# Two-layer trunk on one core: the order of the wide and narrow products inside a k-tile of the feed-forward layers

## The chip, the core and the metric

The kernel runs on one core of a Trainium2 chip. The metric is the device time of one execution in microseconds (us), and of several executions the median is taken. TensorE (PE in the profile) multiplies, and its weight loads are shown apart as PEld; VectorE (DVE), ScalarE (ACT) and GpSimd (POOL) do the element-wise work; SyncE (SP) issues the weight transfers.

## What is computed

The input x is 256 tokens of width 2048 in float32. Two residual layers follow each other, each with a mixer and a feed-forward part, and a final norm ends it. The feed-forward part is where the change lies:

```python
def conv_ffn(h, w_up, conv_w, conv_b, w_down):
    u = jnp.einsum('bsd,df->bsf', h, w_up)          # 2048 -> 11264
    S = u.shape[1]
    y = conv_b
    for tap in range(CONV_WIDTH):
        shifted = jnp.pad(u, ((0, 0), (tap, 0), (0, 0)))[:, :S]
        y = y + shifted * conv_w[CONV_WIDTH - 1 - tap]
    val, gate = jnp.split(y, 2, axis=-1)
    return jnp.einsum('bsf,fd->bsd', jax.nn.silu(gate) * val, w_down)   # 5632 -> 2048

    for l in range(DEPTH):                          # DEPTH = 2
        h = rms_norm(x, mix_norm[l])
        x = x + (parallel_mixer(h, ...) if l % 2 == 0 else pool_mixer(h, ...))
        h = rms_norm(x, ffn_norm[l])
        x = x + conv_ffn(h, w_up[l], conv_w[l], conv_b[l], w_down[l])
    return rms_norm(x, final_norm)
```

## The kernel before

Activations lie feature-major, 128 features on the partitions and 256 tokens (S) along the free axis. Every float32 operand is split in two parts of the type fp32r: a rounded part and the rest. For the weights these are the tiles `hi` (ScalarE, line 727) and `lo` = raw - hi (VectorE, line 1082). For the activations both parts stand side by side in one row of 512 columns, in `h` for the up-projection and in `act` for the down-projection.

A product of a 128x128 block of weights with the activations therefore takes two matmuls. The **wide** one (line 386) multiplies the `hi` block with all 512 columns and writes a whole PSUM bank. The **narrow** one (line 388) multiplies the `lo` block with the first 256 columns and adds to the second half of the same bank. Lo times lo is left out.

A **k-tile** is 128 rows of a weight matrix by 512 columns, so it has four blocks m = 0..3, four banks and eight matmuls. A unit is four k-tiles (KT = 4), which one transfer of 1 MB brings into one of four slots of `raw`. `hi` and `lo` hold one unit each. ScalarE rounds k-tile kt of the next unit when the semaphore `w_used` says that TensorE has done k-tile kt of this one, VectorE then subtracts, and TensorE waits on `lo_done` before each k-tile. `w_used` rises with the last matmul of a k-tile.

In the function `wide_unit` TensorE sends the eight matmuls of a k-tile in alternation: wide 0, narrow 0, wide 1, narrow 1, and so on. It serves the output projection of the first mixer (64 k-tiles), both up-projections (11 pairs of column groups, each 2 x 4 units of 4 k-tiles, so 352 k-tiles for a layer) and both down-projections (4 column groups of 11 units, so 176 k-tiles for a layer). The very last unit is sent by `last_unit` in an order of its own. That makes 352 + 176 k-tiles in the feed-forward part of layer 0 and 352 + 172 in that of layer 1 through `wide_unit`, 1052 together. Two accumulators of four banks alternate from one column group to the next.

Three other orders occur in the kernel. The input projection's queries and keys use `half_unit` (lines 436 and 438), which also alternates wide and narrow. Its value groups and the pool mixer use `token_unit` (lines 468, 470, 471): only matmuls with 512 moving columns, each with another block of weights than the one before. The first group uses `narrow_unit` (lines 452, 454, 455): only matmuls with 256 moving columns. A weight load precedes every matmul.

The up-projections run in a hardware loop over pairs, the down-projection of layer 0 in a loop over two halves; that of layer 1 is written out.

Of the kernel before, what the change touches and what calls it, by code (L numbers as in the profile page):

```python
# [29 lines left out]
P = 128  # L30
# [4 lines left out]
KT = 4  # L35


def trunk_kernel(nc, xT, rel_bias, norm_g, w_in, w_out, lam, subln, pool_w, pool_scale,
                 w_up, conv, w_down, bucket_onehot, rot_cos, rot_sin, decay, pool_matrix, ident_in, flip_in, outT):
    D, S = xT.shape  # L40
# [6 lines left out]
    DN_UNITS = FF // COLS  # L47
    DN_GROUPS = D // COLS
# [65 lines left out]
    with ctx:  # L114
# [174 lines left out]
        def wide_bank(G):  # L289

            return 4 - 4 * (G % 2)
# [83 lines left out]
        def _(pe):  # L375
            def wide_unit(n, base, bank, first, last, moving, ready=None):

                for kt in range(KT):

                    pe.wait_ge(lo_done, base + KT * n + kt + 1)  # L380
                    if ready is not None:
                        ready(kt)
                    mv = moving(kt)
                    for m in range(4):
                        c = slice(m * P, (m + 1) * P)
                        pe.matmul(ps[:, bank + m, :], hi[:, kt, c], mv, start=first and kt == 0, stop=False,  # L386
                                  skip_group_check=True)
                        mm = pe.matmul(ps[:, bank + m, S:2 * S], lo[:, kt, c], mv[:, 0:S], start=False,  # L388
                                       stop=last and kt == KT - 1, skip_group_check=True)
                    mm.then_inc(w_used, 1)  # L390

            def last_unit(n, bank):
# [244 lines left out]
            for l in range(DEPTH):  # L637
                if l == 1:
                    def pool_tokens(g):

                        pe.wait_ge(z_ready, 2 * (g + 1))
                        if g == 0:
                            pe.wait_ge(table_in, 16 * N_TABLE)
                        if g == 1:
                            pe.wait_ge(rms_done, 3)
                        if g >= 2:
                            pe.wait_ge(evacuated, G_POOL + g - 1)
                        z, b = (yv, yg)[g % 2], wide_bank(G_POOL + g) + 2
                        z = z.rearrange("p (t k) s -> p t (k s)", t=2)
                        for m in range(4):  # L650
                            c = slice(m * P, (m + 1) * P)
                            out = ps[:, b + m // 2, (m % 2) * S:(m % 2 + 1) * S]
                            pe.matmul(out[:, 0:NEAR], z[:, 0, c], pool_m[:, g, 0:NEAR], start=m % 2 == 0, stop=False,
                                      skip_group_check=True)
                            mm = pe.matmul(out[:, P:2 * P], z[:, 1, c], pool_m[:, g, S:S + P], start=False, stop=True,
                                           skip_group_check=True)
                        mm.then_inc(pooled_mm, 1)

                    for g in range(4):
                        G = G_POOL + g
# [12 lines left out]
                    pool_tokens(3)  # L675

                def up(i, first):
                    for gt in range(2):
                        G = G_UP[l] + gt
                        pe.wait_ge(evacuated, i * 2 + G - 1)  # L680
                        for j in range(UP_UNITS):
                            def split(kt):
                                pe.wait_ge(h_lo, H_BASE[2 * l + 1] + KT * j + kt + 1)
                            wide_unit(U_UP[l] + 4 * gt + j, i * (8 * KT), wide_bank(G), j == 0, j == UP_UNITS - 1,
                                      lambda kt: h[:, KT * j + kt, :], split if first and gt == 0 else None)
                            if first and gt == 1 and j == 0:
# [8 lines left out]
                def down(i, half, units):  # L695
                    G = G_DN[l] + half
                    pe.wait_ge(evacuated, i * 2 + G - 1)
                    for j in range(units):
                        pe.wait_ge(act_lo, l * PAIRS + j + 1)
                        wide_unit(U_DN[l] + DN_UNITS * half + j, i * (2 * DN_UNITS * KT), wide_bank(G), j == 0,  # L700
                                  j == DN_UNITS - 1, lambda kt: act[:, KT * j + kt, :])

                if l == 0:
                    with pe.Fori(0, DN_GROUPS // 2) as i:
                        down(i, 0, DN_UNITS)
                        down(i, 1, DN_UNITS)
                else:
                    down(0, 0, DN_UNITS)
                    down(0, 1, DN_UNITS)
                    down(1, 0, DN_UNITS)  # L710
                    down(1, 1, DN_UNITS - 1)
# [915 lines left out]
```

## Time and profile before

| | us |
|---|---|
| median of 3 runs | 1962.93 |
| lowest and highest of them | 1962.78, 1976.23 |
| the profiled execution | 1979.08 |
| its span, first to last instruction | 1976.9 |
| busy: PE, DVE, ACT | 1955.4, 1391.7, 1112.8 |

The profile is of one execution, and its own time is 2.2 us longer than its span. A row of the page groups instructions by line, engine and operation: the mean duration of one, the idle time of the engine ahead of them, and what ended it. Matmuls are pipelined, so one that lasts 395 ns in the records can be followed by the next after 233 ns. What a matmul costs is the distance from its start to the next start, called its slot here. The timeline gives starts to 0.01 us, and a slot is best read over several matmuls, or from how many of a kind fall into a stretch.

### The profile page before, as it was taken

The page shows a single profiled execution, that of the slowest core. Times are in us where ns is not written, and L with a number is a line of the kernel's source. Part 1 is how long each engine was busy: PE and PEld are TensorE (multiplying, and loading weights), DVE is VectorE, ACT ScalarE, POOL GpSimd, SP SyncE. Part 2 cuts the span into 40 slices and gives each one's busy share as a digit, 9 for nine tenths or more (in the row PEclk, how much of TensorE's full clock was granted, in tenths as well). Part 3 has the DMA queues.
Part 4 walks back from the last instruction along what each step waited for, and adds up shares of the span by engine and source line. Part 5 has one row for each costly group of instructions (what it writes and reads, how often), then busy time and mean ns, then how long its engine had stood idle before and what let it go on. Part 6 is the DMA issues. An engine that isn't in the chain of part 4 may idle for free.

```text
span 1976.9 us, 31335 instructions
## 1 busy us (share of the span) xinstructions
PE 1955.4 (99%) x11094; PEld 1699.6 (86%) x11094; DVE 1391.7 (70%) x2149; ACT 1112.8 (56%) x1844; POOL 48.2 (2%) x53
## 2 busy tenths in 40 slices
PE   8999999999999999999999999999999999999998
PEld 8888888888888888888888888888888888888887
DVE  6667776767777777777655555877777777755555
ACT  6555545556655666665544445666666656645554
POOL 0002240000000000000000000000000000000000
PEclk9999999999999999999999999999999999999999
DMA  9655555555555555554565554555555555555653
GB/s 321 192 170 164 177 168 164 180 191 186 181 187 191 184 180 188 191 182 159 191 213 181 181 169 150 171 191 191 191 191 191 188 186 187 187 167 191 212 192 107
DMA packets 205203, 364.91 MB, mean 185 GB/s; under 512 B 6564, under 2 KB 49101, under 8 KB 205133
## 3 DMA queue, kind: packets, MB, share of 16 engines
q1 hardware_dynamic: 203388, 362.34, 55.6%
q10 hardware_dynamic: 1744, 1.63, 0.3%
q8 instruction: 46, 0.75, 0.2%
q14 instruction: 25, 0.20, 0.0%
HBM read 361.83 MB, written 2.11 MB: 184 GB/s over the span
## 4 chain that ended last, share of the span: by engine, by line
PE 97%; DVE 2%; ACT 1%; issue 0%; DMA 0%; DVEq 0%; SPq 0%
PE ps L386 53%; PE ps L388 26%; PE ps L436 6%; PE ps L438 3%; PE ps L468 2%; PE ps L471 2%; PE ps L470 2%; DVE lo L1082 1%; PE ps L452 0%; PE ps L454 0%; PE ps L455 0%; ACT hi L727 0%; PE ps L561 0%; PE ps L575 0%; DVE ssq L1200 0%
## 5 line engine op out<-in xcount | busy, mean ns | idle before, releaser
L1082 DVE TENSOR_TENSOR lo<-raw,hi 128x512 fp32r<-128x512 f32 x1360 | 927.8, 698 | 528.7 <-ACT hi L727 524.1
L727 ACT ACTIVATE hi<-raw 128x512 fp32r<-128x512 f32 x1352 | 844.9, 631 | 807.3 <-PE ps L388 672.1
L386 PE MATMUL ps<-h,hi 128*128 128x512 f32 x2816 | 988.5, 397 | 4.8 <-DVE x L1389 3.3
L388 PE MATMUL ps<-h,lo 128*128 128x256 f32 x2816 | 786.5, 279 | 0.0
L386 PEld LDWEIGHTS ps<-h,hi 128*128 128x128 f32 x2816 | 529.4, 188 | 133.6 <-DVE x L1389 3.5
L388 PEld LDWEIGHTS ps<-h,lo 128*128 128x128 f32 x2816 | 531.1, 189 | 0.0
L386 PE MATMUL ps<-act,hi 128*128 128x512 f32 x1392 | 487.3, 396 | 0.0
L388 PE MATMUL ps<-act,lo 128*128 128x256 f32 x1392 | 388.3, 279 | 0.0
L386 PEld LDWEIGHTS ps<-act,hi 128*128 128x128 f32 x1392 | 261.3, 188 | 63.1
L388 PEld LDWEIGHTS ps<-act,lo 128*128 128x128 f32 x1392 | 262.2, 188 | 0.0
L436 PE MATMUL ps<-h,hi 128*128 128x512 f32 x576 | 205.4, 400 | 1.0 <-DVE lo L1082 1.0
L438 PE MATMUL ps<-h,lo 128*128 128x256 f32 x576 | 160.9, 279 | 0.0
L436 PEld LDWEIGHTS ps<-h,hi 128*128 128x128 f32 x576 | 108.1, 188 | 27.2 <-DVE lo L1082 2.1
L438 PEld LDWEIGHTS ps<-h,lo 128*128 128x128 f32 x576 | 108.6, 189 | 0.2
L386 PE MATMUL ps<-mixed,hi 128*128 128x512 f32 x256 | 90.5, 399 | 0.0
L388 PE MATMUL ps<-mixed,lo 128*128 128x256 f32 x256 | 71.9, 281 | 0.0
L468 PE MATMUL ps<-hi,h 128*128 128x512 f32 x160 | 64.4, 403 | 1.2 <-DVE lo L1082 1.0
L470 PE MATMUL ps<-lo,h 128*128 128x512 f32 x160 | 62.9, 393 | 0.0
L471 PE MATMUL ps<-hi,h 128*128 128x512 f32 x160 | 62.9, 393 | 0.0
L1335 DVE TENSOR_TENSOR u<-u,ps 128x1024 f32<-128x1024 f32 x44 | 53.8, 1222 | 9.7 <-ACT u L913 9.7
L386 PEld LDWEIGHTS ps<-mixed,hi 128*128 128x128 f32 x256 | 48.1, 188 | 12.1
L1340 DVE TENSOR_TENSOR u<-u,rstd 128x1024 f32<-128x1024 f32 x44 | 53.9, 1226 | 1.5
(175 smaller groups left out, 1122.4 us busy)
## 6 DMA issues: line engine op xcount, KB each, us to landing
raw<-in_w_up SPq DMA_DIRECT2D x176, 1024.0 KB, 5.0
raw<-in_w_down SPq DMA_DIRECT2D x88, 1024.0 KB, 5.1
raw<-in_w_in SPq DMA_DIRECT2D x54, 1024.0 KB, 5.2
raw<-in_w_out SPq DMA_DIRECT2D x16, 1024.0 KB, 5.0
raw<-in_pool_w SPq DMA_DIRECT2D x4, 1024.0 KB, 5.2
raw<-in_w_in SPq DMA_DIRECT2D x8, 256.0 KB, 4.8
x<-in_xT SPq DMA_DIRECT2D x8, 128.0 KB, 4.6
x<-in_xT SPq DMA_DIRECT2D x2, 512.0 KB, 7.7
```

What stands on the lines that cost most here:

```text
L386: pe.matmul(ps[:, bank + m, :], hi[:, kt, c], mv, start=first and kt == 0, stop=False, skip_group_check=True)
L388: mm = pe.matmul(ps[:, bank + m, S:2 * S], lo[:, kt, c], mv[:, 0:S], start=False, stop=last and kt == KT - 1, skip_group_check=True)
L436: pe.matmul(acc[:, m, :], hi[:, kt, c], mv, start=first and kt == 0 and a == 0, stop=False, skip_group_check=True)
L438: mm = pe.matmul(acc[:, m, S:2 * S], lo[:, kt, c], mv[:, 0:S], start=False, stop=last and kt == KT - 1 and a == 1, skip_group_check=True)
L468: pe.matmul(acc[:, t, :], xh, hi[:, kt, :], start=first and kt == 0, stop=False, skip_group_check=True)
L470: pe.matmul(acc[:, t, :], xh, lo[:, kt, :], start=False, stop=False, skip_group_check=True)
L471: mm = pe.matmul(acc[:, t, :], xl, hi[:, kt, :], start=False, stop=last and kt == KT - 1, skip_group_check=True)
L727: a_.activation(hi[:, kt, :], raw[:, slot, kt, :], ACT.Copy).then_inc(hi_done, 1)
L1082: ve.tensor_tensor(lo[:, kt, :], raw[:, slot, kt, :], hi[:, kt, :].bitcast(F32), ALU.subtract).then_inc(lo_done, 1)
L1335: ve.tensor_tensor(u[:, :, :], u[:, :, :], ps[:, b:b + 4, S:2 * S], ALU.add).then_inc(evacuated, 1)
L1340: ve.tensor_tensor(u[:, :, :], u[:, :, :], rstd_4, ALU.mult).then_inc(u_ready, 1)
```

## The change

The change keeps all matmuls, their operands and their banks. It sets for each stage of the feed-forward layers in which order the eight matmuls of a k-tile are sent. Seven small functions write such orders, and `ordered_unit` takes one of them as an argument. With W for wide and N for narrow, they are:

| order | the eight matmuls | where | k-tiles |
|---|---|---|---|
| rows_then_singles | W0 W1 N0 N1 W2 N2 W3 N3 | up, layer 0 | 352 |
| rows_of_two | W0 W1 N0 N1 W2 W3 N2 N3 | up, layer 1; down, layer 1, groups 1 and 3 | 352 + 44 + 40 |
| folded_end | W0 N0 W1 N1 W2 N2 N3 W3 | down, layer 0 group 0, layer 1 group 2 | 88 |
| row_of_three | W0 W1 W2 N0 N1 N2 W3 N3 | down, layer 0 group 1 | 44 |
| one_ahead | W0 W1 N0 W2 N1 N2 W3 N3 | down, layer 0 group 2 | 44 |
| narrow_first | N0 W0 N1 W1 N2 W2 N3 W3 | down, layer 0 group 3 | 44 |
| one_and_three | W0 N0 W1 W2 W3 N1 N2 N3 | down, layer 1 group 0 | 44 |

In the first k-tile of a group, folded_end and narrow_first keep the old order, since there the wide matmul has to start the bank.

```diff
+            def rows_then_singles(bank, kt, mv, start):
+                wide(bank, kt, 0, mv, start)
+                wide(bank, kt, 1, mv, start)
+                narrow(bank, kt, 0, mv)
+                narrow(bank, kt, 1, mv)
+                wide(bank, kt, 2, mv, start)
+                narrow(bank, kt, 2, mv)
+                wide(bank, kt, 3, mv, start)
+                narrow(bank, kt, 3, mv).then_inc(w_used, 1)
...
+            def rows_of_two(bank, kt, mv, start):
+                for row in (0, 2):
+                    wide(bank, kt, row, mv, start)
+                    wide(bank, kt, row + 1, mv, start)
+                    narrow(bank, kt, row, mv)
+                    mm = narrow(bank, kt, row + 1, mv)
+                mm.then_inc(w_used, 1)
+
+            def ordered_unit(n, base, bank, first, moving, tile, ready=None):
+
+                for kt in range(KT):
+                    pe.wait_ge(lo_done, base + KT * n + kt + 1)
+                    if ready is not None:
+                        ready(kt)
+                    tile(bank, kt, moving(kt), first and kt == 0)
...
-                            wide_unit(U_UP[l] + 4 * gt + j, i * (8 * KT), wide_bank(G), j == 0, j == UP_UNITS - 1,
-                                      lambda kt: h[:, KT * j + kt, :], split if first and gt == 0 else None)
+                            ordered_unit(U_UP[l] + 4 * gt + j, i * (8 * KT), wide_bank(G), j == 0,
+                                         lambda kt: h[:, KT * j + kt, :], (rows_then_singles, rows_of_two)[l],
+                                         split if first and gt == 0 else None)
...
+                down_tiles = ((folded_end, row_of_three, one_ahead, narrow_first),
+                              (one_and_three, rows_of_two, folded_end, rows_of_two))[l]
+                for g in range(DN_GROUPS):
+                    G = G_DN[l] + g
+                    pe.wait_ge(evacuated, G - 1)
+                    for j in range(DN_UNITS - (l == 1 and g == 3)):
                         pe.wait_ge(act_lo, l * PAIRS + j + 1)
-                        wide_unit(U_DN[l] + DN_UNITS * half + j, i * (2 * DN_UNITS * KT), wide_bank(G), j == 0,
-                                  j == DN_UNITS - 1, lambda kt: act[:, KT * j + kt, :])
...
+                        ordered_unit(U_DN[l] + DN_UNITS * g + j, 0, wide_bank(G), j == 0,
+                                     lambda kt: act[:, KT * j + kt, :], down_tiles[g])
```

The down-projection of layer 0 is also written out now, as that of layer 1 was. What the other engines do and their order stay as they were. On TensorE, one k-tile of an up-projection stood like this before (`lo_done` is the semaphore of the tile's `lo` part; REGISTER_ALU works out the value to wait for in the loop):

```order
L380 REGISTER_ALU
L386 MATMUL ps<-h,hi 128x512 [waits lo_done]
L388 MATMUL ps<-h,lo 128x256
L386 MATMUL ps<-h,hi 128x512
L388 MATMUL ps<-h,lo 128x256
L386 MATMUL ps<-h,hi 128x512
L388 MATMUL ps<-h,lo 128x256
L386 MATMUL ps<-h,hi 128x512
L388 MATMUL ps<-h,lo 128x256
```

Wide and narrow alternate through the k-tile and across its border. In the up-projection of layer 0 one k-tile and the start of the next now read (L394 wide, L399 narrow):

```order
L394 MATMUL ps<-h,hi 128x512 [waits lo_done]
L394 MATMUL ps<-h,hi 128x512
L399 MATMUL ps<-h,lo 128x256 x2
L394 MATMUL ps<-h,hi 128x512
L399 MATMUL ps<-h,lo 128x256
L394 MATMUL ps<-h,hi 128x512
L399 MATMUL ps<-h,lo 128x256
L394 MATMUL ps<-h,hi 128x512 [waits lo_done]
L394 MATMUL ps<-h,hi 128x512
```

One narrow has moved behind the next wide, so a wide now follows a wide once and a narrow a narrow once; the other six places are as before. In the up-projection of layer 1 the same piece of TensorE's program reads:

```order
L473 REGISTER_ALU
L394 MATMUL ps<-h,hi 128x512 [waits lo_done]
L394 MATMUL ps<-h,hi 128x512
L399 MATMUL ps<-h,lo 128x256 x2
L394 MATMUL ps<-h,hi 128x512 x2
L399 MATMUL ps<-h,lo 128x256 x2
L473 REGISTER_ALU
L394 MATMUL ps<-h,hi 128x512 [waits lo_done]
```

Here both happen twice. In the down-projection of layer 0, group 0 (folded_end; L421 is the last wide), two k-tiles meet like this:

```order
L394 MATMUL ps<-act,hi 128x512
L399 MATMUL ps<-act,lo 128x256 x2
L421 MATMUL ps<-act,hi 128x512
L394 MATMUL ps<-act,hi 128x512 [waits lo_done,act_lo]
L399 MATMUL ps<-act,lo 128x256
```

The wide that ends one k-tile is followed by the wide that begins the next, and `w_used` now rises with a wide.

## Rows read from the trace of the kernel before

**Rows 1.** The page: busy us (share) xinstructions; PE's granted clock in 40 slices, tenths

```profile
PE 1955.4 (99%) x11094; PEld 1699.6 (86%) x11094; DVE 1391.7 (70%) x2149; ACT 1112.8 (56%) x1844; POOL 48.2 (2%) x53
PEclk9999999999999999999999999999999999999999
PE 97%; DVE 2%; ACT 1%; issue 0%; DMA 0%; DVEq 0%; SPq 0%
```

**Rows 2.** The page's costliest groups: busy us, mean ns | idle before, releaser

```profile
L386 PE MATMUL ps<-h,hi 128*128 128x512 f32 x2816 | 988.5, 397 | 4.8 <-DVE x L1389 3.3
L388 PE MATMUL ps<-h,lo 128*128 128x256 f32 x2816 | 786.5, 279 | 0.0
L386 PE MATMUL ps<-act,hi 128*128 128x512 f32 x1392 | 487.3, 396 | 0.0
```

**Rows 3.** Busy time of line 386 in the four feed-forward stages: us, busy (xinstructions), clock

```profile
353.00:941.00 588.00, 587.80 (x1664) 312.49 (x1663) 1.00 0.56 184
941.00:1189.00 248.00, 248.00 (x703) 131.91 (x702) 1.00 0.56 185
1262.00:1719.00 457.00, 457.00 (x1320) 247.22 (x1319) 1.00 0.57 187
1720.00:1957.00 237.00, 237.00 (x685) 128.17 (x684) 1.00 0.54 183
```

**Rows 4.** The same view of two stretches of 200 us, in layer 0 and layer 1

```profile
700.00:900.00 200.00, 200.00 (x567) 106.35 (x566) 1.00 0.57 185
1500.00:1700.00 200.00, 200.00 (x578) 108.19 (x577) 1.00 0.58 189
```

**Rows 5.** Groups by line from 1500 to 1700 us: the two engines that prepare weights

```profile
L1082 DVE TENSOR_TENSOR lo<-raw,hi 128x512 fp32r<-128x512 f32 x144 | 96.2, 689 | 38.9 <-ACT hi L727 38.9
L727 ACT ACTIVATE hi<-raw 128x512 fp32r<-128x512 f32 x145 | 90.5, 630 | 77.9 <-PE ps L388 77.9
```

**Rows 6.** Timeline of PE, layer 1's first up-projection: start us, us, line, operation

```profile
1258.16 0.40 PE L386 MATMUL ps<-h,hi 128*128 128x512 f32 x1
...
1259.22 0.60 PE L486 MATMUL ps<-sqacc,ones 128*128 128x256 f32 x2
1259.55 0.50 PE L386 MATMUL ps<-h,hi 128*128 128x512 f32 x1
...
1261.05 0.39 PE L386 MATMUL ps<-h,hi 128*128 128x512 f32 x1
...
1263.13 0.39 PE L386 MATMUL ps<-h,hi 128*128 128x512 f32 x1
```

**Rows 7.** Timeline of PE in a token_unit, matmuls of 512 columns alone

```profile
66.75 0.39 PE L468 MATMUL ps<-hi,h 128*128 128x512 f32 x1
...
69.47 0.39 PE L468 MATMUL ps<-hi,h 128*128 128x512 f32 x1
```

**Rows 8.** Timeline of PE in a narrow_unit, matmuls of 256 columns alone

```profile
19.50 0.28 PE L452 MATMUL ps<-h,hi 128*128 128x256 f32 x1
...
21.66 0.28 PE L452 MATMUL ps<-h,hi 128*128 128x256 f32 x1
```

**Rows 9.** Timeline of PE where a token_unit is followed by a half_unit

```profile
228.40 0.39 PE L471 MATMUL ps<-hi,h 128*128 128x512 f32 x1
228.63 0.39 PE L436 MATMUL ps<-h,hi 128*128 128x512 f32 x1
228.85 0.28 PE L438 MATMUL ps<-h,lo 128*128 128x256 f32 x1
228.97 0.40 PE L436 MATMUL ps<-h,hi 128*128 128x512 f32 x1
...
229.32 0.40 PE L436 MATMUL ps<-h,hi 128*128 128x512 f32 x1
...
229.68 0.40 PE L436 MATMUL ps<-h,hi 128*128 128x512 f32 x1
```

**Rows 10.** Timeline of PE where alternation is followed by a token_unit

```profile
1189.88 0.40 PE L468 MATMUL ps<-hi,h 128*128 128x512 f32 x1
1190.12 0.40 PE L470 MATMUL ps<-lo,h 128*128 128x512 f32 x1
...
1191.98 0.39 PE L468 MATMUL ps<-hi,h 128*128 128x512 f32 x1
```

More of the change, by code:

```diff
@@ L390, in wide_unit, with wide, narrow @@
                     mm.then_inc(w_used, 1)
+            def wide(bank, kt, m, mv, start=False):
+                pe.matmul(ps[:, bank + m, :], hi[:, kt, m * P:(m + 1) * P], mv, start=start, stop=False,
+                          skip_group_check=True)
+            def narrow(bank, kt, m, mv):
+                return pe.matmul(ps[:, bank + m, S:2 * S], lo[:, kt, m * P:(m + 1) * P], mv[:, 0:S], start=False,
+                                 stop=False, skip_group_check=True)
+            def rows_then_singles(bank, kt, mv, start):
[7 more added lines that the diff above has]
+                narrow(bank, kt, 3, mv).then_inc(w_used, 1)
@@ new lines, in folded_end @@
+            def folded_end(bank, kt, mv, start):
+                for m in range(3):
+                    wide(bank, kt, m, mv, start)
+                    narrow(bank, kt, m, mv)
+                if start:
+                    wide(bank, kt, 3, mv, start)
+                    narrow(bank, kt, 3, mv).then_inc(w_used, 1)
+                else:
+                    narrow(bank, kt, 3, mv)
+                    pe.matmul(ps[:, bank + 3, :], hi[:, kt, 3 * P:4 * P], mv, start=False, stop=False,
+                              skip_group_check=True).then_inc(w_used, 1)
@@ new lines, in row_of_three, with one_ahead @@
+            def row_of_three(bank, kt, mv, start):
+                for m in range(3):
+                    wide(bank, kt, m, mv, start)
+                for m in range(3):
+                    narrow(bank, kt, m, mv)
+                wide(bank, kt, 3, mv, start)
+                narrow(bank, kt, 3, mv).then_inc(w_used, 1)
+            def one_ahead(bank, kt, mv, start):
+                wide(bank, kt, 0, mv, start)
+                wide(bank, kt, 1, mv, start)
+                narrow(bank, kt, 0, mv)
+                wide(bank, kt, 2, mv, start)
+                narrow(bank, kt, 1, mv)
+                narrow(bank, kt, 2, mv)
+                wide(bank, kt, 3, mv, start)
+                narrow(bank, kt, 3, mv).then_inc(w_used, 1)
@@ new lines, in one_and_three, with narrow_first @@
+            def one_and_three(bank, kt, mv, start):
+                wide(bank, kt, 0, mv, start)
+                narrow(bank, kt, 0, mv)
+                for m in range(1, 4):
+                    wide(bank, kt, m, mv, start)
+                for m in range(1, 4):
+                    mm = narrow(bank, kt, m, mv)
+                mm.then_inc(w_used, 1)
+            def narrow_first(bank, kt, mv, start):
+                for m in range(4):
+                    if start:
+                        wide(bank, kt, m, mv, start)
+                        mm = narrow(bank, kt, m, mv)
+                    else:
+                        narrow(bank, kt, m, mv)
+                        mm = pe.matmul(ps[:, bank + m, :], hi[:, kt, m * P:(m + 1) * P], mv, start=False, stop=False,
+                                       skip_group_check=True)
+                mm.then_inc(w_used, 1)
@@ new lines, in rows_of_two @@
+            def rows_of_two(bank, kt, mv, start):
[4 more added lines that the diff above has]
+                    mm = narrow(bank, kt, row + 1, mv)
+                mm.then_inc(w_used, 1)
+            def ordered_unit(n, base, bank, first, moving, tile, ready=None):
[4 more added lines that the diff above has]
+                    tile(bank, kt, moving(kt), first and kt == 0)
@@ L694, in _ @@
                     up(i, False)
[L695 to L698, printed above, removed]
-                        pe.wait_ge(act_lo, l * PAIRS + j + 1)
-                        wide_unit(U_DN[l] + DN_UNITS * half + j, i * (2 * DN_UNITS * KT), wide_bank(G), j == 0,
-                                  j == DN_UNITS - 1, lambda kt: act[:, KT * j + kt, :])
[L703 to L711, printed above, removed]
+                down_tiles = ((folded_end, row_of_three, one_ahead, narrow_first),
[4 more added lines that the diff above has]
+                    for j in range(DN_UNITS - (l == 1 and g == 3)):
+                        pe.wait_ge(act_lo, l * PAIRS + j + 1)
+                        ordered_unit(U_DN[l] + DN_UNITS * g + j, 0, wide_bank(G), j == 0,
+                                     lambda kt: act[:, KT * j + kt, :], down_tiles[g])
+                if l == 1:
                     last_unit(U_DN[1] + DN_UNITS * DN_GROUPS - 1, wide_bank(G_DN[1] + 3))
```

## The prediction

> **What bounds the kernel now.** I read the page's engine shares first. TensorE is busy for 99% of the span, the chain that ended last lies on it for 97%, and its clock is at the full level in every slice [rows 1]. In the page's costliest groups the wide matmuls of lines 386 and 388 had 4.8 us of idle time ahead of them in all, most of it in front of one layer's start, and the narrow ones none [rows 2]. So neither a transfer nor a preparing engine sets the pace of the feed-forward parts; TensorE's own rate does. From 1500 to 1700 us, 144 or 145 k-tiles pass. VectorE idles 38.9 us for ScalarE in them, and ScalarE 77.9 us for TensorE's release of a k-tile [rows 5]. ScalarE thus waits about 0.5 us per k-tile for TensorE, never the other way round.
>
> A busy share says nothing about the rate, so I counted matmuls per stretch. A wide and a narrow make a pair, and there are four in a k-tile. From 700 to 900 us 567 wides start, 352.7 ns for a pair. From 1500 to 1700 us there are 578, 346.0 ns for a pair [rows 4]. It is the same code with the same shapes, no waits and the full clock. The four stages show that the rate goes by layer: 588.0 us / 1664 = 353.4 ns and 248.0 / 703 = 352.8 ns in layer 0, 457.0 / 1320 = 346.2 ns and 237.0 / 685 = 346.0 ns in layer 1 [rows 3]. The loop or the written-out form makes no difference: the last stage is written out, the one before it is a loop, and both run at 346.
>
> So **alternation has two steady rates**, 353 and 346 ns a pair, and keeps the one it falls into. The timeline shows it change. From 1258.16 to 1259.22 us three pairs took 1.06 us, 353 each. Then two small matmuls of line 486 interrupt the stream, and from 1261.05 to 1263.13 six pairs took 2.08 us, 346.7 each [rows 6]. What an interruption changes must be how the starts fall against something inside the engine; the trace doesn't show what.
>
> **What equal neighbours cost.** The change puts a wide behind a wide and a narrow behind a narrow, which alternation never does. The trace has both in other stages. Twelve 512-column matmuls in a row, each with another weight block, took 69.47 - 66.75 = 2.72 us, 226.7 ns each [rows 7]. Eighteen 256-column ones took 21.66 - 19.50 = 2.16 us, 120.0 ns each [rows 8]. Together that is 346.7 ns for one wide and one narrow, the faster rate of alternation. The 256 columns between the two shapes take 106.7 ns, 2.4 a nanosecond, which leaves 13.3 ns on top for each matmul of either shape. The pure streams and the good alternation pay the same.
>
> The Trainium skill, page "TensorE: Matmul & The Clock Gate", section "Back-to-back issue gap", gives N / 2.4 + 2.5 ns from start to start at the full clock, so 215.8 and 109.2 ns. The rows above, at 226.7 and 120.0, differ from it by 11 ns each. By the page's figures an equal neighbour would be cheaper than any slot this kernel shows. I go by the rows.
>
> **The change part by part.** Counting wide-to-wide places with the next k-tile's first matmul included, rows_of_two, row_of_three and one_and_three have 2 in a k-tile, rows_then_singles, one_ahead and folded_end 1, narrow_first 0. Layer 0 has 352 x 1 + 44 x (1 + 2 + 1 + 0) = 528 of them. Layer 1 has 352 x 2 + 44 x (2 + 2 + 1) + 40 x 2 = 1004. Together 1532, and as many narrow-to-narrow. Each such couple replaces a wide-to-narrow and a narrow-to-wide.
>
> *Slots.* In layer 1, which is at the faster rate, one couple costs 226.7 + 120.0 in place of 346.0, so +0.7 ns, and over all 1532 of them +1.1 us. In layer 0 I take it that the new orders do not hold the slower rate: each k-tile there breaks the alternation at least once (narrow_first apart), and the slower rate is seen only in unbroken alternation. Then 528 k-tiles x 4 pairs x (352.7 - 346.0 = 6.7 ns) = -14.2 us.
>
> *Bounds of a slot.* The nearest rows to a change of neighbours are the places where stages meet. Behind a stream of wides, the first two alternating pairs took 229.32 - 228.63 = 0.69 us, 345 each, and the third 0.36 us [rows 9]. That is the cheap end, 1.7 ns a pair under the fast rate. Behind slow alternation, a stream of wides needs ten matmuls to settle: 1191.98 - 1189.88 = 2.10 us for nine, 233.3 ns each, 6.6 over the settled 226.7 [rows 10]. That is the dear end. I take the settled price, because it agrees from three sides, and keep both ends.
>
> *k-tile's end.* narrow_first and folded_end let `w_used` rise with a wide in place of a narrow. It still is the last of the same eight, so it comes when the k-tile is through. ScalarE's half microsecond of waiting per k-tile [rows 5] covers any shift of one slot. Without that cover, a shift of 0.1 us would reach TensorE by way of `lo_done`. Cost nothing.
>
> *Written-out loop, register work.* Two groups more of TensorE's code are written out in layer 0, at nothing, as rows 3 show for layer 1.
>
> **The sum.** The profiled execution took 1979.1 us. 1979.1 - 14.2 + 1.1 = **1966.0 us**. Two of the three runs of before are at 1962.8 and one at 1976.2; the 13.4 us between them are what one layer at the slower rate costs. So the median 1962.9 is probably already a run with both layers at the faster rate, and against it the change brings +3, 0.2%. About 1% is what a measurement of this kernel can tell from no change, so this is no change.
>
> **The rivals.**
>
> *A: the mixtures fall into a slow rate of their own.* Breaking a steady alternation may as well land in the dear rate as in the cheap one: rows 6 show that an interruption decides, not which way. With 352.7 ns a pair everywhere the time is 1966.0 + 1052 x 4 x 6.7 ns = 1966 + 28 = 1994, 1.6% slower. Half of the k-tiles there, or each k-tile half way, gives 1980. For it speaks that the pairs behind a stream of wides did not stay cheap: the third took 360 ns [rows 9]. Against it speaks that two of the new orders' pieces, the pure rows, have one rate only.
>
> *B, the other side by more: the stream never settles.* In rows 10 the starts need ten matmuls to settle after a change of neighbours, and the new orders have a change of neighbours within every eight. If each slot stays 6.6 ns dear, a k-tile costs 53 ns more and the time is 1966 + 1052 x 53 ns = 2022. It turns from no change to slower where a k-tile costs more than 16 ns over 1387, since 1982.6 - 1966 = 16.6 us over 1052 k-tiles. Against it: the ladder in rows 10 starts from the slow rate, and its excess shrinks.
>
> *C: equal neighbours are cheap inside a k-tile.* Here a wide following a wide goes to another bank and keeps its moving columns, which no stage of before does; in rows 7 the bank stays. If both slots lost 10.9 ns, 1532 couples would give 1532 x 21.9 = 33 us, so 1933, and with the wides alone 1949. Those are the gaps that the Trainium skill's section "Back-to-back issue gap" gives. By rows, only the 1.7 ns a pair of rows 9 can be won: 1052 x 4 x 1.7 = 7 us, so 1959. In rows 8 three narrows share bank and weight block and still take 120, which speaks against a saving.
>
> *D: nothing changes, layer by layer.* The rate of each layer is again drawn at its start, the orders do nothing: 1963 to 1979, as before. It differs from my forecast in the trace, not in the verdict.
>
> **How the numbers follow.** The forecast and D together, 1962 to 1970 and with one slow layer 1979, have a chance of 0.50. A in full has 0.15, A by half 0.12, B 0.10, C in full 0.05, and the small gain of rows 9 0.08. Slower by over 1% (above 1982.6) takes A in full, B, and the upper end of A by half: 0.26. Faster by over 1% (below 1943.3) is C and a little of the untried ground beside it: 0.07. The rest, 0.67, is no change. The range runs from 1950, which leaves out C in full, to 1994, which takes in A in full and leaves out B: 0.85 by the cases, the rest being for what I haven't thought of.
>
> **What the changed profile would show.** Right: 346 to 348 ns a pair in all four stages when wides are counted per stretch, whatever the order, and wide-to-wide 227 and narrow-to-narrow 120 in the timeline. A: 353 in some stages, a rate that goes by order and not by layer. B: 358 or more, most in rows_of_two, with wide-to-wide starts of 231 to 240 ns. C: wide-to-wide starts of 216. The stage of narrow_first is a check on all of it: it still alternates, so it must show either 346 or 353. Wrong in another way would be idle time of TensorE ahead of the k-tiles' first matmul, which would mean that `lo_done` comes late, and then ScalarE's idle time would have gone.

## The result and the profile after

| | before | after |
|---|---|---|
| median, 20 runs each | 1975.05 us | 1977.98 us |
| lowest, highest | 1962.78, 1992.96 | 1974.29, 1980.35 |
| the profiled execution | 1979.08 us | 1978.38 us |

The ratio of after to before is 1.0037, with a 95% interval from 1.0021 to 1.0054: slower by 0.4%, less than the 1% that I had called telling. It leaves out the run of before at 1993.0 us as a slow one; the medians of all 20 differ by 0.15%. The spread says more than the medians. The 20 runs of before stand in three heaps: nine from 1962.8 to 1965.7, ten from 1974.4 to 1979.5, one at 1993.0. The 20 runs of after stand in one, 6 us wide. The three runs that I had to predict from held two of the low heap, so their median, 1962.9, was not the kernel's.

The kernel before was run 73 times more beside the experiments, in three sets: 18 times from 1960.1 to 1966.3, 45 times from 1973.4 to 1981.2 and 10 times from 1988.9 to 1994.3. All 93 together have a median of 1977.6 and a mean of 1975.4. So the 0.4% also depends on which mix of heaps stood against the change; against all 93 it is between nothing and 0.2%. The changed kernel itself was timed only in the first set.

The page of after hardly differs from that of before. TensorE is as full, its clock as high, the chain as much its own as in [rows 1], and the idle time ahead of the wide matmuls is still the 4.8 us of [rows 2]:

```profile
PE 1954.9 (99%) x11094; PEld 1702.0 (86%) x11094; DVE 1390.9 (70%) x2149; ACT 1110.3 (56%) x1844; POOL 48.1 (2%) x53
PEclk9999999999999999999999999999999999999999
PE 97%; DVE 2%; ACT 1%; issue 0%; DMA 0%; DVEq 0%; SPq 0%
L394 PE MATMUL ps<-h,hi 128*128 128x512 f32 x2816 | 914.6, 397 | 4.8 <-DVE x L1469 3.3
```

The rate is what changed. This is the busy time of the narrow matmuls (line 399) in the up-projections of layer 0 and layer 1, with their number behind the x, as [rows 3] had it for the wide ones:

```profile
443.00:938.00 495.00, 337.67 (x1407) 266.06 (x1407) 1.00 0.56 184
1262.00:1716.00 454.00, 256.04 (x1304) 244.78 (x1304) 1.00 0.56 186
```

That is 495.0 us / 1407 = 351.8 ns a pair for rows_then_singles, 1407 ns a k-tile, and 454.0 / 1304 = 348.2 ns for rows_of_two, 1393 ns a k-tile. Before, a k-tile took 1413 or 1387 ns (353.3 and 346.7 a pair). The first rate is better than the dear one and worse than the good one, the second likewise. The timeline of PE gives the down-projection's orders. The last wide of folded_end, eleven k-tiles apart:

```profile
949.50 0.40 PE L421 MATMUL ps<-act,hi 128*128 128x512 f32 x1
...
965.05 0.40 PE L421 MATMUL ps<-act,hi 128*128 128x512 f32 x1
```

The row of three wides in row_of_three, ten k-tiles apart:

```profile
1010.42 0.86 PE L394 MATMUL ps<-act,hi 128*128 128x512 f32 x3
...
1024.43 0.86 PE L394 MATMUL ps<-act,hi 128*128 128x512 f32 x3
```

And narrow_first, three pairs apart:

```profile
1144.75 0.39 PE L458 MATMUL ps<-act,hi 128*128 128x512 f32 x1
...
1145.79 0.39 PE L458 MATMUL ps<-act,hi 128*128 128x512 f32 x1
```

These are 15.55 / 11 = 1.413 us a k-tile, 14.01 / 10 = 1.401, and 1.04 / 3 = 347 ns a pair, so 1387. From the starts of all matmuls of each stage, to the nanosecond, the steady k-tiles are these. In row_of_three and one_and_three the slots repeat only every four k-tiles, in one_ahead every two, and the mean is given:

| order | ns a k-tile | over 1386.7 | k-tiles | us |
|---|---|---|---|---|
| rows_then_singles | 1406.7 | 20.0 | 352 | 7.0 |
| rows_of_two | 1393.3 | 6.7 | 436 | 2.9 |
| folded_end | 1413.3 | 26.7 | 88 | 2.3 |
| row_of_three, one_ahead, one_and_three | 1400.0 | 13.3 | 132 | 1.8 |
| narrow_first | 1386.7 | 0 | 44 | 0.0 |

The last column adds up to 14.0 us over a kernel in which every k-tile takes 1386.7.

### The profile page after: what moved, and what is told of

It is laid out like the page before. It is cut to its first block, busy times and chain, and to the rows that moved or that the text cites. A ratio compares the mean times of both kernels' runs of the same rounds, so it can differ in the third digit from the quotient of the medians.

```text
span 1976.3 us, 31190 instructions
## 1 busy us (share of the span) xinstructions
PE 1954.9 (99%) x11094; PEld 1702.0 (86%) x11094; DVE 1390.9 (70%) x2149; ACT 1110.3 (56%) x1844; POOL 48.1 (2%) x53
## 4 chain that ended last, share of the span: by engine, by line
PE 97%; DVE 2%; ACT 1%; issue 0%; DMA 0%; DVEq 0%; SPq 0%
PE ps L394 47%; PE ps L399 25%; PE ps L522 6%; PE ps L524 3%; PE ps L386 3%; PE ps L458 2%; PE ps L554 2%; PE ps L556 2%; PE ps L557 2%; PE ps L388 2%; PE ps L421 1%; DVE lo L1162 1%; PE ps L538 0%; PE ps L540 0%; PE ps L541 0%; ACT hi L807 0%
## 5 line engine op out<-in xcount | busy, mean ns | idle before, releaser
L394 PE MATMUL ps<-h,hi 128*128 128x512 f32 x2816 | 914.6, 397 | 4.8 <-DVE x L1469 3.3
L399 PE MATMUL ps<-h,lo 128*128 128x256 f32 x2816 | 615.4, 280 | 0.0
L399 PEld LDWEIGHTS ps<-h,lo 128*128 128x128 f32 x2816 | 531.5, 189 | 93.0
L394 PEld LDWEIGHTS ps<-h,hi 128*128 128x128 f32 x2816 | 456.4, 189 | 38.5 <-DVE x L1469 3.5
L394 PE MATMUL ps<-act,hi 128*128 128x512 f32 x1134 | 369.1, 396 | 0.0
L399 PE MATMUL ps<-act,lo 128*128 128x256 f32 x1392 | 312.1, 280 | 0.0
L399 PEld LDWEIGHTS ps<-act,lo 128*128 128x128 f32 x1392 | 255.7, 188 | 35.1
L394 PEld LDWEIGHTS ps<-act,hi 128*128 128x128 f32 x1134 | 192.1, 188 | 19.9
L522 PE MATMUL ps<-h,hi 128*128 128x512 f32 x576 | 206.0, 401 | 0.9 <-DVE lo L1162 0.9
L524 PE MATMUL ps<-h,lo 128*128 128x256 f32 x576 | 161.2, 280 | 0.0
L522 PEld LDWEIGHTS ps<-h,hi 128*128 128x128 f32 x576 | 108.2, 188 | 27.5 <-DVE lo L1162 2.0
L458 PE MATMUL ps<-act,hi 128*128 128x512 f32 x172 | 59.7, 391 | 0.0
```

The lines of the kernel that those rows point to most:

```text
L394: pe.matmul(ps[:, bank + m, :], hi[:, kt, m * P:(m + 1) * P], mv, start=start, stop=False, skip_group_check=True)
L399: return pe.matmul(ps[:, bank + m, S:2 * S], lo[:, kt, m * P:(m + 1) * P], mv[:, 0:S], start=False, stop=False, skip_group_check=True)
L458: mm = pe.matmul(ps[:, bank + m, :], hi[:, kt, m * P:(m + 1) * P], mv, start=False, stop=False, skip_group_check=True)
L522: pe.matmul(acc[:, m, :], hi[:, kt, c], mv, start=first and kt == 0 and a == 0, stop=False, skip_group_check=True)
L524: mm = pe.matmul(acc[:, m, S:2 * S], lo[:, kt, c], mv[:, 0:S], start=False, stop=last and kt == KT - 1 and a == 1, skip_group_check=True)
```

## The experiments

I read the spread of before as a lottery of alternation, and the one narrow heap of after as a sign that the new orders have none. Two theories stood at the start. By **theory O** a k-tile's rate is a property of the order. By **theory D** it is drawn when a stage begins. Two more asked for the cause: the banks (B, not the rival of that letter), and a price for each equal neighbour. `by_order`, in the diffs, sends the eight matmuls of a k-tile as a string says, and in the first k-tile of a column group alternates. The diffs are shortened. The runs from narrow_first to rows_of_four, folded_end and the rotated banks are built on the kernel before, with the down-projection of layer 0 written out as in the change and the same string for all stages.

### One order everywhere: narrow_first

```diff
-                (rows_then_singles, rows_of_two)[l]
+                by_order("N0 W0 N1 W1 N2 W2 N3 W3")
-                                     down_tiles[g])
+                                     by_order("N0 W0 N1 W1 N2 W2 N3 W3"))
```

> All ten feed-forward stages send N0 W0 N1 W1 N2 W2 N3 W3 (the first k-tile of a column group in the old order). Outside the feed-forward k-tiles the kernel spends 505.5 us: 1978.4 less 352 x 1407.1, 44 x (1412.7 + 1400.3 + 1400.0 + 1386.7), 352 x 1393.3, 44 x (1400.4 + 1413.1) and 84 x 1393.4 ns, the means of the changed kernel's stages. Theory O (each order of shapes has a steady rate of its own, and narrow_first's is 1386.7 ns a k-tile): every stage at 1387, 505.5 + 1052 x 1.3867 = 1964 us in every round. Theory D (narrow_first is alternation, and the rate of alternation is drawn at the start of a layer or group): some groups at 1387 and some at 1413, times between 1964 and 1992 that differ from round to round, as the kernel before does.

Measured: 1986.02 us, 12 runs from 1982.9 to 1987.7, ratio 1.0052 (1.0025 to 1.0079). Both theories failed. Not every group ran at 1387, and yet the rounds agreed within 5 us. Group by group, the up-projections ran at 1413, all but two groups of each layer: the second, inside which the norm's small matmuls fall, and the third, right behind it. (The first group of layer 1 still has waits in it and is left aside.) The four down-projection groups of both layers ran at 1413, 1387, 1413, 1387, the same series twice. That is no drawing of lots.

In this kernel each group but the first begins with a wide behind a wide, alternates for a k-tile, and then has one narrow behind a narrow (the row with x2). Here is the timeline of PE at that place, for a group that went on at 1413:

```profile
941.16 0.40 PE L417 MATMUL ps<-act,hi 128*128 128x512 f32 x1
941.40 0.28 PE L408 MATMUL ps<-act,lo 128*128 128x256 f32 x1
941.52 0.40 PE L417 MATMUL ps<-act,hi 128*128 128x512 f32 x1
941.75 0.40 PE L408 MATMUL ps<-act,lo 128*128 128x256 f32 x2
941.99 0.40 PE L417 MATMUL ps<-act,hi 128*128 128x512 f32 x1
```

And for the next group, which went on at 1387:

```profile
1003.33 0.40 PE L417 MATMUL ps<-act,hi 128*128 128x512 f32 x1
1003.57 0.28 PE L408 MATMUL ps<-act,lo 128*128 128x256 f32 x1
1003.68 0.40 PE L417 MATMUL ps<-act,hi 128*128 128x512 f32 x1
1003.92 0.40 PE L408 MATMUL ps<-act,lo 128*128 128x256 f32 x2
1004.16 0.40 PE L417 MATMUL ps<-act,hi 128*128 128x512 f32 x1
```

The difference is small. From the last wide ahead of the two narrows to the wide behind them it is 0.47 us in the first and 0.48 in the second. To the nanosecond, the two slots ahead of the second narrow are 235, 113 in the first and 241, 120 in the second. Slow alternation is a cycle of three pairs, 236 + 113, 233 + 117 and 241 + 120, which makes 1060 ns. Fast alternation is 346.7 a pair, as 230 + 117 or as 231 + 112 and 233 + 117. So the disturbance met the cycle at another point. All 43 groups with 236, 113 there, within a nanosecond, and no interruption behind it went on at 1413, and all four with 241, 120 at 1387. The two third groups came in at the fast rate with 230, 116 or 117 there, and stayed fast. An up group has 60 pairs between disturbances, a multiple of three, a down group 172, which is not, and this fits the series. **Theory M** came of it: the slots follow a fixed map, and what an interruption does depends on where in the cycle it falls.

### One order everywhere: rows_of_two, rows_of_four, folded_end

The same edit with another string. First rows_of_two:

> All feed-forward stages send W0 W1 N0 N1 W2 W3 N2 N3. Theory O: 1393.3 ns a k-tile in every stage and layer, as in layer 1 of the changed kernel; 505.5 + 1052 x 1.3933 = 1971 us, rounds within 2 us. Theory D: layer 0 differs from layer 1, by up to 26 ns a k-tile, and the rounds spread.

Measured: 1971.07 us, 10 runs from 1968.6 to 1972.7, ratio 0.9977 (0.9943 to 1.001). Theory O hit it: 1393 ns in all stages, in layer 0 too. From 500 to 700 and from 1500 to 1700 us, 1149 matmuls start:

```profile
500.00:700.00 200.00, 200.00 (x1149) 174.39 (x1147) 156.50 (x243) 121.14 (x198) 0.00 (x0) 1.00 0.58 187
1500.00:1700.00 200.00, 200.00 (x1149) 174.41 (x1148) 156.34 (x243) 121.14 (x198) 0.00 (x0) 1.00 0.55 182
```

Then W0 W1 W2 W3 N0 N1 N2 N3, which was not in the change:

> All feed-forward stages send W0 W1 W2 W3 N0 N1 N2 N3, the order with the most equal neighbours: three wide behind a wide and three narrow behind a narrow in a k-tile. Equal neighbours cheap (rival C): fewer ns than rows_of_two's 1393, below 1387. Settled price for every slot (my prediction): 1387, 1964 us. Theory X (each change between wide-led and narrow-led running costs a few ns until it settles, rival B): 1400 or more, as row_of_three and one_and_three showed, 1978 us or more.

Measured: 1982.17 us in 8 runs, 1403 ns a k-tile (1401 and 1406 by turns) in every stage. The settled price and rival C both fell: the order with the most equal neighbours is dearer than rows_of_two, which has fewer, and cheaper than rows_then_singles, which has fewer still.

> All feed-forward stages send folded_end, W0 N0 W1 N1 W2 N2 N3 W3, with one wide-to-wide and one narrow-to-narrow neighbour in a k-tile. Theory O: 1413 ns a k-tile everywhere, 505.5 + 1052 x 1.4133 = 1992 us, the dearest of the orders although it has fewer equal neighbours than rows_of_two with 1393. A price per equal neighbour, whatever the order around it: one neighbour of each kind costs +20 ns in rows_then_singles (1407) and half of rows_of_two's +6.7, which can't both hold; by the first, 1407 ns and 1985 us.

Measured: 1990.62 us in 8 runs, ratio 1.0080 (1.0041 to 1.0119), with 1413 ns a k-tile. With one couple of equal neighbours folded_end costs 27 ns over the good rate, rows_then_singles with one couple 20, rows_of_two with two 7, rows_of_four with three 17. **A price for each equal neighbour does not exist**; the whole sequence has a rate.

### The layers exchanged

```diff
-                                         lambda kt: h[:, KT * j + kt, :], (rows_then_singles, rows_of_two)[l],
+                                         lambda kt: h[:, KT * j + kt, :], (rows_of_two, rows_then_singles)[l],
-                down_tiles = ((folded_end, row_of_three, one_ahead, narrow_first),
-                              (one_and_three, rows_of_two, folded_end, rows_of_two))[l]
+                down_tiles = ((one_and_three, rows_of_two, folded_end, rows_of_two),
+                              (folded_end, row_of_three, one_ahead, narrow_first))[l]
```

> The changed kernel with the orders of the two layers exchanged: layer 0 gets rows_of_two up and one_and_three, rows_of_two, folded_end, rows_of_two down, layer 1 rows_then_singles up and folded_end, row_of_three, one_ahead, narrow_first down. Theory O (the rate belongs to the order, not to the stage): rows_of_two 1393, rows_then_singles 1407, folded_end 1413, row_of_three, one_ahead and one_and_three 1400 ns a k-tile in their new places, and 1978 us in all, within 2; only narrow_first, which alternates, may stand at 1387 or 1413 (1.1 us). A theory by which layer 0 is the slow layer: rates go by place, the total changes.

Measured: 1979.18 us, 10 runs from 1975.6 to 1980.2. The rates moved with the orders: 1393, 1400, 1393, 1413, 1393 in layer 0 and 1407, 1413, 1400, 1400, 1387 in layer 1. In the counts, layer 0 now has the larger number of matmuls in 200 us and layer 1 the smaller:

```profile
700.00:900.00 200.00, 200.00 (x1151) 174.51 (x1150) 156.26 (x243) 121.09 (x198) 0.00 (x0) 1.00 0.58 187
1300.00:1500.00 200.00, 200.00 (x1139) 174.62 (x1138) 154.50 (x238) 119.19 (x194) 0.00 (x0) 1.00 0.58 187
```

### The banks

```diff
-                by_order("W0 N0 W1 N1 W2 N2 W3 N3")
+                by_order("W0 N3 W1 N0 W2 N1 W3 N2")
```

> Alternation of the shapes as before (written out in layer 0), but a narrow goes to another bank than the wide ahead of it: W0 N3 W1 N0 W2 N1 W3 N2. Theory S (only the sequence of shapes matters): the two rates of alternation, 1387 and 1413 ns a k-tile, in some mix, 1964, 1978 or 1992 us. Theory B (a wide followed by a narrow into the same bank pays for it): the 241 ns wide-to-narrow slots vanish, a k-tile at 1387 or less everywhere.

Measured: 1975.96 us, 10 runs, four of them from 1961.6 to 1965.4 and six from 1975.1 to 1980.7. These are the heaps of before. In the profiled run layer 0 fell into the fast rate and layer 1 into the slow one, the other way round than in [rows 4]:

```profile
700.00:900.00 200.00, 200.00 (x1155) 174.89 (x1155) 157.06 (x245) 121.00 (x198) 0.00 (x0) 1.00 0.58 189
1500.00:1700.00 200.00, 200.00 (x1133) 173.52 (x1132) 154.57 (x239) 119.47 (x195) 0.00 (x0) 1.00 0.54 178
```

Both rates exist though no narrow follows a wide into its bank, apart from the first k-tile of each group. So a narrow that writes to the bank of the wide ahead of it is not what makes the second rate. The run also speaks for what the heaps are. Its profiled execution took 1978.05 us with one slow layer, and that of before 1979.08 with one. A slow layer costs 528 k-tiles x 26.7 ns = 14 us, so none, one or both would make 1964, 1978 and 1992; the next two runs show the two ends.

### Steering alternation

If M holds, the good rate can be forced. The orders of the change help: rows_then_singles has one steady cycle of exactly one k-tile, which ends in 241, 120 at its border. A narrow right behind that is the disturbance that led to 1387.

```diff
+            def steered(bank, kt, mv, start, first, gt, j):
+                if not first or (gt, j) == (1, 3):
+                    name = KICK if first and kt == 0 else "narrow_first"
+                elif gt == 1 and j > 0:
+                    name = "rows_then_singles"
+                else:
+                    name = "alternate"
+                by_order(name)(bank, kt, mv, start)
```

`KICK` is "narrow_first" here. In the first k-tile of a group the narrow matmul starts the bank, and the down-projections send narrow_first throughout.

> Alternation in all feed-forward stages, but steered into its faster rate once a layer. In the first pair of column groups, behind the small matmuls of the norm, eight k-tiles go in rows_then_singles, whose steady slots end 241, 120 at a k-tile's border. From there on every k-tile is narrow_first, with the narrow matmul starting the bank, so that one narrow-to-narrow neighbour stands right behind the 120 slot and none follows for the rest of the layer. Theory M (the sequence of slots is a fixed map: the same neighbours at the same point of the cycle lead to the same rate; in the run with narrow_first everywhere, a narrow-to-narrow behind 241, 120 led to 1387 in each of the four groups where it stood there): 1387 ns a k-tile in both layers in every round, 505.5 + 1052 x 1.3867 + 16 x 0.020 = 1965 us, spread as small as rows_of_two's. Theory D (drawn anew each time): a mix of about 1964, 1978 and 1992 us as before.

Measured: 1964.75 us, 12 runs from 1962.0 to 1966.4, ratio 0.9954 (0.9934 to 0.9974). All narrow_first stages of both layers ran at 1386.7. It beats the kernel before by 0.5% in the runs beside it, and its median lies 0.7% under that of the changed kernel, which was timed in another set. It is no faster than the lowest heap of before; it always lands there. The control moves the kick by one pair, with W0 N0 N1 W1 N2 W2 N3 W3 as the k-tile that brings it:

```diff
-KICK = "narrow_first"
+KICK = "one_pair_later"
```

> The steered kernel with the narrow-to-narrow neighbour one pair later: the k-tile behind rows_then_singles is W0 N0 N1 W1 N2 W2 N3 W3, so it stands behind 236, 113 and not behind 241, 120. Everything else is the same. Theory M: behind 113 a narrow-to-narrow led to 1413 in all groups of the run with narrow_first everywhere, so both layers at 1413 ns a k-tile and 1965 + 28 = 1992 us in every round. Theory D, or a theory that the narrow-led order itself is fast: the same time as the steered kernel.

Measured: 1991.8 us, 6 runs from 1990.5 to 1994.4, ratio 1.0093 (1.0063 to 1.0124). All stages at 1413. The two kernels differ in the place of one narrow matmul in each layer, and by 27 us. In layer 0 their slots stay within a nanosecond of each other through the eight k-tiles of rows_then_singles ahead of it. In both timelines of PE the row with x2 is the place. Steered:

```profile
483.54 0.40 PE L419 MATMUL ps<-h,hi 128*128 128x512 f32 x1
483.78 0.40 PE L422 MATMUL ps<-h,lo 128*128 128x256 f32 x2
484.02 0.40 PE L419 MATMUL ps<-h,hi 128*128 128x512 f32 x1
...
486.10 0.40 PE L419 MATMUL ps<-h,hi 128*128 128x512 f32 x1
```

One pair later:

```profile
483.57 0.40 PE L419 MATMUL ps<-h,hi 128*128 128x512 f32 x1
483.81 0.40 PE L422 MATMUL ps<-h,lo 128*128 128x256 f32 x2
484.04 0.40 PE L419 MATMUL ps<-h,hi 128*128 128x512 f32 x1
...
486.16 0.40 PE L419 MATMUL ps<-h,hi 128*128 128x512 f32 x1
```

Six pairs later the first has used 2.08 us (347 a pair) and the second 2.12 (353), and so it goes on for the rest of the layer. 1156 matmuls against 1135 start from 1500 to 1700 us:

```profile
1500.00:1700.00 200.00, 200.00 (x1156) 174.90 (x1155) 157.24 (x245) 122.45 (x200) 0.00 (x0) 1.00 0.56 184
```

```profile
1500.00:1700.00 200.00, 200.00 (x1135) 173.35 (x1134) 154.43 (x240) 119.25 (x195) 0.00 (x0) 1.00 0.57 187
```

### The size of the narrow matmul

These two start from the kernel before and change one line. They leave the rest of the computation as it is.

```diff
-                        mm = pe.matmul(ps[:, bank + m, S:2 * S], lo[:, kt, c], mv[:, 0:S], start=False,
+                        mm = pe.matmul(ps[:, bank + m, S:S + 128], lo[:, kt, c], mv[:, 0:128], start=False,
```

> The kernel before, with the narrow matmul of the feed-forward and output-projection k-tiles cut to 128 columns (the lo part of the weights is left out for half of the tokens). Theory L (a slot is never shorter than the weight load behind it, and 120 ns is that load): a narrow slot stays at 120, a k-tile near 1387 ns, about 1964 us. Theory F (each matmul costs its columns at 2.4 a nanosecond and a fixed 13.3): 53.3 + 13.3 = 66.7 ns for the narrow, 1173 ns a k-tile, about 1740 us.

Measured, one run: 1932.55 us, and 1360 ns a k-tile in every group, 340 a pair. The timeline of PE shows 280 and 60 ns slots:

```profile
600.06 0.44 PE L386 MATMUL ps<-h,hi 128*128 128x512 f32 x1
600.34 0.22 PE L388 MATMUL ps<-h,lo 128*128 128x128 f32 x1
600.40 0.44 PE L386 MATMUL ps<-h,hi 128*128 128x512 f32 x1
```

Neither theory hit the size. Half the columns of the narrow matmul saved 6.7 ns of a pair against the faster rate instead of the 53.3 of theory F. With 226.7 for the wide, 113.3 ns are left for a matmul whose columns take 53.3, so something other than columns holds the pair. L names a candidate, the weight load behind the short matmul, and is nearer, though the narrow's own slot is 60 ns and not 120. The trace's weight loads speak for it. They start at 600.00, 600.11, 600.34 and 600.45 us, by turns 108 and 232 ns apart. The load for the narrow starts 52 ns behind the wide ahead of it, where in the kernel before it starts 2 to 5 ns behind. So the narrow's load seems to be held up until 108 ns after the load before it. The Trainium skill, page "TensorE: Matmul & The Clock Gate", section "LDWEIGHTS (loading the stationary operand)", puts a load at P / 1.2 ns for P columns. For 128 columns that is an estimate of 106.7 ns. The 108 ns between two loads agree with it; the loads' own records last 188 to 191 ns. No run isolates the load.

For 384 columns the same line reads `ps[:, bank + m, 128:512]` and `mv[:, 0:384]`.

> The kernel before, with the narrow matmul of the same k-tiles widened to 384 columns (128 of them added to the wrong sums, so its result differs). Both theories give 160 + 13.3 = 173.3 ns for it and 1600 ns a k-tile, 505.5 + 1052 x 1.600 = 2189 us. If the second, slower rate comes from a narrow matmul that is as short as the weight load behind it (106.7 against 120), it is gone here and all k-tiles cost 1600; if it comes from alternating two shapes as such, some stages cost more, by about 27 ns.

Measured, one run: 2257.99 us. A k-tile took 1627 ns through the output projection and at the start of layer 0. The rate changes between 488 and 492 us, where the norm's small matmuls fall, and from there on it is 1653. Starts of two wides four pairs apart:

```profile
399.64 0.39 PE L386 MATMUL ps<-mixed,hi 128*128 128x512 f32 x1
...
401.26 0.39 PE L386 MATMUL ps<-mixed,hi 128*128 128x512 f32 x1
```

```profile
599.87 0.40 PE L386 MATMUL ps<-h,hi 128*128 128x512 f32 x1
...
601.52 0.40 PE L386 MATMUL ps<-h,hi 128*128 128x512 f32 x1
```

That is 1.62 against 1.65 us. Two rates again, 406.7 and 413.3 a pair, and both are above the 400.0 that columns and 13.3 ns a matmul give. The shortness of the narrow matmul does not make the second rate, since its slot here, 175 ns, is longer than the 108 that two loads kept apart above. Alternating two shapes costs by itself, 6.7 or 13.3 ns a pair here, none or 6.7 with 256 columns.

## Why the prediction was right or wrong

**What bounds the kernel, right.** TensorE's own rate sets the time; neither transfers nor ScalarE nor VectorE do. After the change ScalarE still waits for TensorE about half a microsecond for each k-tile, and the idle time ahead of the matmuls is the same 4.8 us.

**Alternation has two steady rates, right**, and the reading that the heaps of the runs are slow layers was right too: forced both ways, the kernel took 1964.75 and 1991.8 us. But I had three runs, two of them low, and took 1962.9 for the base. The next 17 runs of before show that one slow layer is at least as common as none. Against the median of 20, 1975, my 1966 was a gain of 0.5%, and the change is a loss of 0.4% by the ratio, 0.15% by the medians. The profiled execution, at 1979, should have told me that the forecast lay under a usual time of the kernel. That two of my three runs were low was the luck of the draw: of 93, 27 are.

**"Slots: one couple costs 226.7 + 120.0 in place of 346.0", wrong.** This is the step that failed, with its twin for layer 0, that "the new orders do not hold the slower rate", so that every pair there costs 346. I priced each place by the settled rate of a stream of its kind, as if nothing carried over from one place to the next, and took the agreement of three numbers for enough. This is TensorE in rows_then_singles:

```profile
600.86 0.62 PE L394 MATMUL ps<-h,hi 128*128 128x512 f32 x2
601.32 0.40 PE L399 MATMUL ps<-h,lo 128*128 128x256 f32 x2
601.55 0.40 PE L394 MATMUL ps<-h,hi 128*128 128x512 f32 x1
601.79 0.28 PE L399 MATMUL ps<-h,lo 128*128 128x256 f32 x1
601.91 0.40 PE L394 MATMUL ps<-h,hi 128*128 128x512 f32 x1
602.15 0.28 PE L399 MATMUL ps<-h,lo 128*128 128x256 f32 x1
602.27 0.62 PE L394 MATMUL ps<-h,hi 128*128 128x512 f32 x2
```

The half with both equal neighbours took 0.69 us, the half that alternates 0.72. To the nanosecond the slots are 236, 227, 113, 119 and then 234, 117, 241, 120, so 695 and 712, where I had about 693 for each. The equal neighbours cost nearly what I said, and the pairs that I took as settled did not. With 236 + 113, 234 + 117 and 241 + 120 all three pairs of the slow cycle are in this k-tile, about 1060 ns, and one pair of 346 besides. In the same way folded_end is the slow cycle and one pair of 353. So one break in a k-tile does not seem to undo the slow cycle; that is a reading of the slots, and no run tests it. In rows_of_two, with two couples, no such cycle can be picked out, and it costs 6.7 ns.

Over the whole kernel the term was +1.1 us, and measured, the new orders cost 14.0 us over 1386.7 everywhere. 1966.0 - 1.1 + 14.0 = 1978.9 us, which is the measured 1978.0 within a microsecond. By layer, the -14.2 us of layer 0 came out as -14.2 + 9.4 = -4.8: 7.0 from rows_then_singles, 1.2 from folded_end, 1.2 from row_of_three and one_ahead. Layer 1, at 1387 in the profile of before, rose by 4.7: 2.9 from rows_of_two, 1.2 from folded_end, 0.6 from one_and_three.

**Two readings of rows, wrong without consequence.** Line 388 is the narrow matmul, and the 4.8 us of [rows 2] belong to line 386 alone. In [rows 8] only two of the three narrows that follow each other share a weight block, the third takes `lo`.

**The rivals.** A by half, "each k-tile half way, gives 1980", was what happened, and I gave it 0.12. Its reason held as well: after a disturbance the pairs did not stay cheap. It is rather a rate for each order between the two than a mix of both. B was right in kind, the slots don't settle within eight, and two to eight times too dear: 7 to 27 ns a k-tile in place of 53. Some slots came out under the settled price too, such as 113 for a narrow in place of 120, which the first pair of [rows 9] already had. And rows_of_two, where B expected most, was among the cheapest. C fell: no order went below 1386.7, with rows_of_four tried for it, and the wide-to-wide slots were never 216, but 224 at the least in the steady stages. That also decides against the isolated gap that the Trainium skill gives in "TensorE: Matmul & The Clock Gate", section "Back-to-back issue gap", for this kernel's type of matmul. D is refuted by the 6 us spread of after and by the exchange of the layers, where the rates moved with the orders.

**Written-out loop, k-tile's end, ScalarE's cover, right**: the written-out and looped rows_of_two both ran at 1393.

**The range** held 1978, and no change by over 1%, which I gave 0.67, is what came. Against the base as it turned out, the direction was wrong.

## What to carry to other kernels

When TensorE is full, count the matmuls in equal stretches before pricing a reorder: the same code can run at two rates, and a median of three runs may be one side of a coin. Do not price a sequence of unequal matmuls by its neighbours; measure the sequence as a whole, best with each order in a stage of its own, as this changed kernel does. Where a stream has two rates, look for the disturbance that starts it, and place it, rather than look for a better order.

## What the runs showed of the hardware

- A stream of alternating 512- and 256-column fp32r matmuls, each with its weight load, has two self-sustaining rates at the full clock, 346.7 and 353.3 ns a pair, and keeps them for thousands of matmuls (almost 4000 in layer 0 of the steered kernel).
- The slots repeat within a nanosecond or two. A narrow behind a narrow led to the slow rate behind slots of 236, 113 and to the fast one behind 241, 120, in every group where nothing else interrupted, and one narrow matmul moved by one pair in each layer decided 27 us.
- The steady k-tiles of nearly all orders are multiples of 6.67 ns, some as the mean of two or four k-tiles: 1360.0, 1386.7, 1393.3, 1400.0, 1406.7, 1413.3, 1626.7 and 1653.3. In rows_of_four it is two k-tiles together, 2806.7 ns. What in the engine has that step is open. A narrow in the bank of the wide ahead of it is excluded as the cause, the stage and the loop form too, and so is the shortness of the narrow matmul as the only cause. Whether the weight load's timing or the order of reads behind it makes the two rates was not tried. In the profile of before the loads start 2 to 5 ns behind the matmul ahead of them at either rate.
- A narrow matmul cut from 256 to 128 columns saved 6.7 ns of the pair against the faster rate, not 53.
